# A two-block transformer kernel on one core: the front's first steps in another order

## The reference

```python
c_act = jax.nn.silu(c)
mod = c_act @ w_ada + b_ada                                # w_ada: 2048 x 6144
shift, scale, gate = jnp.split(mod, 3, axis=-1)
h = rms_norm(x, g) * (1.0 + scale[:, None]) + shift[:, None]
proj = jnp.einsum('bsd,df->bsf', h, w_in)                  # w_in: 2048 wide, chunks 0 to 9 of 512 columns in the front
```

## Time and profile before

| | |
|---|---|
| median of 3 runs | 1444.6 us (1443.38 to 1445.47) |
| the profiled execution's own time | 1443.75 us |
| its span | 1441.6 us |
| PE busy | 98% of the span |
| DVE busy | 83% |
| ACT busy | 49% |
| granted TensorE clock, mean | 0.996 |
| DMA over the span | 450.97 MB, mean 313 GB/s |

### The profile page before, as it was taken

The page is one execution under the profiler, slowest core; times in us unless marked ns, Lnnn a source line. Parts: engine busy times, 40 slices in busy tenths (PEclk is TensorE's granted clock), DMA queues, the critical chain, the costliest instruction groups (busy, mean ns, idle before and its releaser), DMA issues.

```text
span 1441.6 us, 19793 instructions
## 1 busy us (share of the span) xinstructions
PE 1406.3 (98%) x6934; PEld 1175.4 (82%) x6934; DVE 1191.0 (83%) x1533; ACT 708.5 (49%) x1039; POOL 139.9 (10%) x233
## 2 busy tenths in 40 slices
PE   6999999999999999999999999999999999999996
PEld 4778888878887788888888888878888888888885
DVE  6899899887999889898878789888887877677566
ACT  5564434754444644444455553464345545465440
POOL 1111011002100001110011101010010002110000
PEclk9999999999999999999999999999999999999999
DMA  9999999878997899999977799689789688775762
GB/s 355 411 412 416 411 404 385 311 284 280 403 415 259 288 347 379 406 377 359 347 237 255 239 343 406 195 279 360 262 338 345 209 311 270 231 252 173 266 194 97
DMA packets 101625, 450.97 MB, mean 313 GB/s; under 512 B 11730, under 2 KB 16162, under 8 KB 77858
## 3 DMA queue, kind: packets, MB, share of 16 engines
q1 hardware_dynamic: 68690, 247.63, 48.0%
q0 software_dynamic: 25584, 185.63, 33.4%
q10 hardware_dynamic: 7264, 16.55, 3.5%
HBM read 447.62 MB, written 2.15 MB: 312 GB/s over the span
## 4 chain that ended last, share of the span: by engine, by line
PE 84%; DVE 7%; DMA 4%; issue 3%; ACT 2%; POOL 0%; DVEq 0%; SPq 0%; ACTq 0%
PE bank L862 15%; PE bank L879 15%; PE bank L881 15%; PE bank L880 14%; PE bank L860 8%; DVE gw L1660 3%; PE bank L814 3%; PE bank L816 3%; PE bank L815 3%; DMA raw<-in_t_steps 3%; PE bank L1109 2%; PE bank L1067 2%; DVE w_lo L1652 2%; PE bank L858 1%; PE bank L827 1%
## 5 line engine op out<-in xcount | busy, mean ns | idle before, releaser
L1190 ACT CAST w_hi<-raw 128x1024 fp32r<-128x1024 f32 x436 | 457.4, 1051 | 610.0 <-PE bank L881 282.7
L1635 DVE TENSOR_TENSOR w_lo<-raw,w_hi 128x1024 fp32r<-128x1024 f32 x360 | 438.7, 1226 | 179.1 <-ACT w_hi L1190 177.7
L1660 DVE CUSTOM_DVE_ANT_0 gw<-gw,c_act 128x2048 f32<-128x2048 f32 x176 | 402.4, 2287 | 0.0
L880 PE MATMUL bank<-w_lo,act_parts 128*128 128x512 f32 x1024 | 398.9, 390 | 0.0
L879 PE MATMUL bank<-w_hi,act_parts 128*128 128x512 f32 x960 | 386.4, 403 | 0.5 <-issue 0.5
L881 PE MATMUL bank<-w_hi,act_parts 128*128 128x512 f32 x960 | 374.9, 391 | 0.0
L862 PE MATMUL bank<-act_parts,w_hi 128*128 128x512 f32 x960 | 338.3, 395 | 0.0
L860 PE MATMUL bank<-act_parts,w_lo 128*128 128x256 f32 x1024 | 276.9, 281 | 0.0
L880 PEld LDWEIGHTS bank<-w_lo,act_parts 128*128 128x128 f32 x1024 | 192.6, 188 | 38.2
L862 PEld LDWEIGHTS bank<-act_parts,w_hi 128*128 128x128 f32 x960 | 180.1, 188 | 39.1
L881 PEld LDWEIGHTS bank<-w_hi,act_parts 128*128 128x128 f32 x960 | 180.2, 188 | 38.8
(11 more groups left out here) (197 smaller groups left out, 1060.2 us busy)
## 6 DMA issues: line engine op xcount, KB each, us to landing
raw<-in_t_steps SPq DMA_DIRECT2D x464, 512.0 KB, 6.3
gw<-in_t_mod POOLq DMA_DIRECT2D x96, 1024.0 KB, 8.2
gw<-in_t_ada POOLq DMA_DIRECT2D x48, 1024.0 KB, 8.3
gw<-in_t_kv_mod POOLq DMA_DIRECT2D x32, 1024.0 KB, 8.0
area<-gate_rows ACTq DMA_DIRECT2D x3, 1024.0 KB, 13.3
bias<-forget_sums ACTq DMA_DIRECT2D x16, 192.0 KB, 5.7
area<-in_ln_g ACTq DMA_DIRECT2D x2, 1024.0 KB, 9.2
area<-in_ln_b ACTq DMA_DIRECT2D x2, 1024.0 KB, 13.0
```

The costliest lines, as they stand in the source:

```text
L880: nc.tensor.matmul(dst, hi, w_lo[:, j % SLOTS, k], start=False, stop=False)
L1190: nc.scalar.copy(w_hi[:, b], raw[:, j % SLOTS]).then_inc(hi_ready, 1)
L1635: nc.vector.tensor_tensor(w_lo[:, j % SLOTS], raw[:, j % SLOTS], w_hi[:, j % LEAD].bitcast(F32), ALU.subtract).then_inc(lo_ready, 1)
L1660: nc.vector.tensor_tensor_reduce(out=w, in0=w, in1=c_act[:].rearrange("p (t n) -> p t n", t=TT), scale=1.0, scalar=0.0, op0=ALU.mult, op1= ...
```

## The change

The tables of the front and a few places in the opening are written anew. The first step is now (2, 0), (4, 0), the second (0, 0), (1, 0), the third (3, 0), (5, 0): three steps of k-tile 0. Chunks 2 and 4 are parted after one k-tile in place of two, so their banks are closed with step 0. Then steps take two chunks of one k-tile in many places where they took one chunk of two k-tiles. The row blocks, low parts and shifts have other places; the first two row blocks wait for the spread of c in place of the first part of x; raw loads 0 to 3 wait for row block 0, and the fifth for block 2; block 2 is issued when block 1 has landed.

```diff
-PARTED = {0: 8, 1: 8, 2: 2, 4: 2, 3: 2, 5: 2, 8: 4, 6: 8, 9: 6, 7: 8}
-PART_BANKS = ({0: 0, 1: 1, 2: 2, 4: 3, 3: 2, 5: 3, 8: 2, 6: 3, 9: 2, 7: 2},
-              {2: 0, 4: 1, 3: 3, 5: 2, 0: 0, 1: 1, 8: 0, 9: 1, 6: 0, 7: 1})
-FRONT = [((0, 0), (1, 0)), ((2, 0), (4, 0)), ((2, 1), (4, 1)), ((0, 1), (1, 1))]
...
+PARTED = {0: 8, 1: 8, 2: 1, 4: 1, 3: 2, 5: 2, 8: 4, 6: 8, 9: 6, 7: 8}
+PART_BANKS = ({2: 0, 4: 1, 0: 2, 1: 3, 3: 0, 5: 1, 8: 0, 6: 1, 9: 0, 7: 0},
+              {2: 2, 4: 3, 3: 1, 5: 0, 0: 0, 1: 1, 8: 0, 9: 1, 6: 0, 7: 1})
+FRONT = [((2, 0), (4, 0)), ((0, 0), (1, 0)), ((3, 0), (5, 0)), ((3, 1), (5, 1)), ((0, 1), (1, 1)), ((8, 0), (8, 1)),
+         ((6, 0), (6, 1))]
+FRONT += [((p, kt), (q, kt)) for kt in (2, 3) for p, q in ((8, 6), (0, 1))]
...
+FRONT += [((2, 1), (4, 1))] + [((q, kt), (q, kt + 1)) for q in (2, 4, 3, 5) for kt in (2, 4, 6)]
+FRONT += [((p, kt), (q, kt)) for kt in range(8, KT) for p, q in ((2, 4), (3, 5))]
...
-ROW_AT = {4: 4, 5: 5, 6: 6, 7: 7, 8: 9, 9: 10, 10: 12, 11: 13, 12: 15, 13: 16, 14: 18, 15: 20}
-ROW_AT.update({g: 22 + int((g - 16) * 1.65) for g in range(16, HEAD_TILES)})
-LOW_AT = {1: 2, 2: 6, 3: 8, 4: 12, 5: 14, 6: 18, 7: 21}
+ROW_AT = {3: 2, 4: 4, 5: 5, 6: 6, 7: 8, 8: 10, 9: 11, 10: 13, 11: 14, 12: 16, 13: 18, 14: 20, 15: 21}
+ROW_AT.update({g: 23 + int((g - 16) * 1.65) for g in range(16, HEAD_TILES)})
+LOW_AT = {1: 3, 2: 6, 3: 9, 4: 12, 5: 15, 6: 19, 7: 22}
...
-SHIFT_AT = {1: 3}
-SHIFT_AT.update({kt: ROW_AT[2 * kt + 1] + (3 if kt < 8 else 2) for kt in range(2, KT)})
+SHIFT_AT = {1: 3, 2: 6, 3: 10, 4: 13, 5: 17, 6: 21, 7: 24}
+SHIFT_AT.update({kt: ROW_AT[2 * kt + 1] + 2 for kt in range(8, KT)})
...
             for k in range(FRONT_STEPS):
-                if k == 2:
+                if k == 0:
+
+                    sp.wait_ge(gw_landed[0], 16)
+                if k == LEAD:
 
                     sp.wait_ge(gw_landed[2], 16)
...
-            pool.wait_ge(x_begun, 16)
+            pool.wait_ge(c_spread, 2)
             load(0)
             load(1)
             inverse_root(("x",))
 
-            pool.wait_ge(raw_landed[0], 16)
+            pool.wait_ge(gw_landed[1], 16)
...
-                if n < 2:
-                    pe.wait_ge(head_kept, 4 * (n + 1))
...
+                    if n < 2:
+
+                        pe.wait_ge(head_kept, 2 * (bank_of(q, 0) + 1))
...
             head_step(0)
-            for r in range(6):
+            for r in range(2):
                 head_keep(r)
             head_kt(0)
-            for r in range(6, TURNS):
+            head_step(1)
+            for r in range(2, TURNS):
                 head_keep(r)
-            head_step(1)
...
+                gemv_step(0)
                 dve.wait_ge(root_ready, 1)
                 nc.vector.tensor_scalar(area[:, Q, 1], resid[:, 1], rstd[:, 1:2], None, ALU.mult
                                         ).then_inc(xhat_ready, 1)
+                gemv_step(1)
                 dve.wait_ge(vecs_landed, 16)
-                gemv_step(0)
-                gemv_step(1)
                 head_finish(0)
                 split_low(0)
                 head_low(0)
                 split_low(1)
                 gemv_step(2)
-                gemv_step(3)
-                head_finish(1)
```

More of the change, by code:

```diff
@@ new lines @@
+PART_BANKS = ({2: 0, 4: 1, 0: 2, 1: 3, 3: 0, 5: 1, 8: 0, 6: 1, 9: 0, 7: 0},
[3 more added lines that the diff above has]
+FRONT += [((p, kt), (q, kt)) for kt in (2, 3) for p, q in ((8, 6), (0, 1))]
+FRONT += [((9, kt), (9, kt + 1)) for kt in (0, 2)]
+FRONT += [((p, kt), (q, kt)) for kt in (4, 5) for p, q in ((9, 6), (0, 1))]
@@ L122 @@
+FRONT += [((7, kt), (7, kt + 1)) for kt in (0, 2, 4)]
+FRONT += [((p, kt), (q, kt)) for kt in (6, 7) for p, q in ((0, 1), (6, 7))]
+FRONT += [((2, 1), (4, 1))] + [((q, kt), (q, kt + 1)) for q in (2, 4, 3, 5) for kt in (2, 4, 6)]
+FRONT += [((p, kt), (q, kt)) for kt in range(8, KT) for p, q in ((2, 4), (3, 5))]
+FRONT += [((q, kt), (q, kt + 1)) for q in (0, 1, 8, 9, 6, 7) for kt in range(PARTED[q], KT, 2)]
 FRONT_STEPS = len(FRONT)
 HEAD_LEAD, LEAD_STEPS = 6, 24
-ROW_AT = {4: 4, 5: 5, 6: 6, 7: 7, 8: 9, 9: 10, 10: 12, 11: 13, 12: 15, 13: 16, 14: 18, 15: 20}
@@ L626, in _ @@
             sp.dma_start(vecs[:], a["t_vecs"]).then_inc(vecs_landed, 16)
-            sp.wait_ge(x_landed[1], 32)
             def decay_load(n):
@@ L1503, in head_x @@
                 spread_silu(1)
+                spread_silu(2)
                 act.wait_ge(x_begun, 16)
@@ L1507, in head_x @@
                                      accum_out=square_sums[:, 0:1]).then_inc(x_squared, 1)
-                spread_silu(2)
                 spread_silu(3).then_inc(silu_ready, 1)
@@ L1730, in front @@
                             head_low(kt)
-                    for g in range(4, HEAD_TILES):
+                    for g in range(3, HEAD_TILES):
                         if ROW_AT[g] == m:
```

## The result

| | before | after |
|---|---|---|
| median | 1444.6 us (9 runs, 1443.12 to 1448.76) | 1452.14 us (9 runs, 1450.23 to 1456.49) |
| the profiled execution | 1443.75 us, span 1441.6 | 1452.83 us, span 1451.0 |

After stands to before as 1.0051, with a 95% interval of 1.004 to 1.0062: the change costs 7.5 us. The forecast was 1442.2 with a range of 1439.6 to 1445.2, most likely no difference that can be told, and slower only with 0.06. It was wrong, on the side that I held least likely, and my slower rival is not what happened.

What follows compares the result with a forecast made beforehand. PE, busy 1406.3 of 1441.6 us, could win only idle or low-clock time, with full DMA engines bounding the front; the front's lead, cut to 2.4 us, took 1443.75 to 1441.3, median 1442.2, range 1439.6 to 1445.2.

Steps and rivals of the forecast that it cites:

- my slower rival: Opening: raw loads beside blocks 2 and 3 delay block 3's landing and so step 2; 1446.5 us at 31 us; chance 0.08.
- the rest: Other banks for the parts, PE's waits on kept copies, SP's removed wait on x: claimed to cost nothing.
- what is kept of it: Steps 52 to 61: bytes limit the lead, the hole gives 2.1 us; step 61 starts 2.0 to 3.0 earlier, 2.4 taken.
- The opening: Start of the front: x lands 0.8 us earlier, and step 0 starts at 21.0, 0.9 us earlier.
- The third step: Step 2, k-tile 0 again: waits for `parted` behind k-tile 1's scaling, starts at 31.5 against 32.05, pays 1.6 us low clock.
- the late variant: Opening: step 0's raw load late, delaying all by a microsecond; step 2 starts at 32.6, lead at step 8 is 1.6 us.
- K-tile 2: Steps 2 to 7: low part at 40.9 against 45.16, DVE wins about 4 us; steps end at 50.0, 2.7 us ahead.
- my own signs of being wrong: Step 2 right behind step 1, no longer wait near step 61, block 3 landing after 29, step 8's lead under 1 us.
- One k-tile a step: Middle of the front: only small stalls at steps 15 and 22; PE 3 to 4 us ahead at step 50.
- the cap by bytes: At step 52 bytes, not PE, bind: its load can land earlier only by the hole's 2.1 us, less a short dip.
- the first: Rival on the front's end: all of the 3 to 4 us stays, plus 0.7 at step 61; 1440.3 us; chance 0.27.
- The third: Rival on the opening: block 3 lands after some 29 us, each further microsecond delays step 2; 1446.5 us; chance 0.08.

Runs made afterwards that it cites:

- experiment 5: Changed kernel, but ACT copies the banks of chunks 2 and 4 before k-tile 1's pair: 1452.26 us, ratio 1.0051 to the kernel before.
- experiment 6: experiment 2 with the edit of experiment 5 (bank copies of chunks 2 and 4 ahead of k-tile 1's scaling): 1442.44 us, ratio 0.998.
- experiment 8: experiment 2 with the opening's transfers in the old order, row blocks and raw loads waiting as before: 1445.22 us, ratio 1.0004.
- experiment 9: experiment 2 with only SP's waits, which hold the raw loads, put back as before: 1445.1 us, ratio 1.0002.
- experiment 2: Changed kernel with the old bank table and k-tiles 8 to 15 again two at a time through one chunk: 1441.76 us, ratio 0.9981.
- experiment 1: Changed kernel with only the old table of banks put back: 1448.79 us, ratio 1.0025 to the kernel before.
- experiment 7: experiment 2 with the row blocks of steps 48 to 63 begun four steps later: 1443.25 us, ratio 0.9979.
- experiment 11: experiment 2 with the edits of experiment 5 and experiment 7 together: 1442.98 us, ratio 0.9986.

## Why the prediction was wrong

Point by point, by its own steps.

*The step that failed* is the one called **the rest**: "other banks for the parts [...] costs nothing: each is met when its neighbour is". I had asked for the waits on kept copies at the beginning of the front, where I looked at `parted` with care and found that step 2 stands behind k-tile 1's pair, and did not ask the same of `evacuated` at its end. The other half of the same mistake stands under **what is kept of it**: "adds now come in two steps of four in place of four of two, the same sum". The sum was right, 4.8 us for these four chunks' adds in both (a fifth chunk's two adds, at 197.70 in before, fall into the stretch too). But PE waits for one add in the list and not for the sum, and that one moved from the first place (177.4) to the last (185.7). No rival had it either. Measured, the two together are 10.4 us (1452.14 against 1441.76; 10.0 if each is taken against before's median in its own group), 3.4 for the banks and 7.0 for the order, taken away one after the other. The new banks with the old order were not run.

*The opening*: forecast 0.9 us earlier for step 0, measured later. It starts at 22.30 against 21.92. x did not land earlier by the row blocks' later start (DVE's square of its half is at 9.63 us in both), so the 0.8 us that I had estimated for it has no support in these traces. PE's 32 transposes began at 16.26 and took 6.29 us where they took 5.10. Why they took longer is not shown; in experiment 5, whose lists are the same up to there, they took 5.56 us and step 0 started at 21.36.

*The third step*: right in its mechanism, `parted` behind k-tile 1, which held step 2 until 33.06 (forecast 31.5, and 32.6 in the late variant). Block 3 was in time: DVE's work on it began at 27.22, straight after a split. Block 2 came at 23.86, for which DVE waited 1.75 us; that held back the split of step 2 and block 3 behind it, and is the size of the 1.6 us by which step 2 missed its forecast. The low clock cost more than taken: all twelve matmuls of the step ran at the slow pace, 33.06 to 38.3, where before it ended within the step.

*K-tile 2*: low part at 42.34, where 40.9 to 42.3 was forecast: right in the late variant. But steps 2 to 7 did not end at 50.0 (51.1 in the late variant): step 8 starts at 52.14 against 52.72, **0.6 us ahead where I had 2.7**. Of the 2.1 us missing, 1.6 are the later start of step 2, and its longer low clock accounts for the rest. A lead under 1 us at step 8 was one of my own signs of being wrong, and it came.

*One k-tile a step*: DVE's list in the middle of the front held as walked; PE was 1.3 to 1.9 us ahead in steps 11 to 52 wherever a cast that waits for PE tells it in both, where I had 3 to 4. What k-tiles 2 to 7 gain by it was not measured apart. Its end, k-tiles 8 to 15, is where the loss arises: alone on the kernel before it costs 5.0 us.

*What is kept*: experiments 5, 6, 8 and 9 and the table bear out the cap by bytes, and with the bank wait taken away the sum came out at its size: 2.4 us forecast, 2.5 measured (0.9981). That the size fits so well is in part luck, since its terms do not. The hole at 16 to 19 us was filled, but 0.2 MB or so of it only moved, to 14 to 16 us (338 GB/s where before had 393) and 8 to 10. The load of step 52 was cast at 167.35 in place of 168.34, 1.0 us earlier where I had 2.1 and more, in the profiled execution. Nor did the surplus go where I had it go: PE's waits between steps 53 and 61 in experiment 2 are 0.63 and 0.65 us, not 1.5 to 2.

*The rivals*: the first (the gain survives to the end) found no support: more lead than the bytes give never came out in a median. The third, block 3 landing late, did not occur. As for the rule of the Trainium skill ("DMA: Bandwidth & Descriptors", Queues, rings and completion order) that each engine takes turns between its queues: the trace of after agrees. Block 2, now with raw loads beside it, took 8.5 us from issue to landing where it took 5.2 before; that is the slower rival in a milder form, 1.75 us of DVE's time and no more. As for the low clock: experiment 5 keeps the granted clock at 1.00 in 28 to 40 us, where after has 0.72, but the wait and the low clock then fall on step 5, and the time stays the same.

## What to carry to other kernels

When a change moves where accumulators close, go through each opening of a new part and ask which closed one its banks come from, at which place in the adding engine's list that one is read, and when that place is reached in the trace of before: here the answer, adds that end at 186.6 us against a start at 177.8, was in rows of a trace already at hand. Equal sums of work on an engine say nothing about the one item in its queue that another engine waits for. And where the transfers look like the bound of a stretch, as here, it was the edits that start transfers earlier that paid, and a PE that waited less was no gain by itself.

## What the runs showed of the hardware

The slow pace behind a wait of PE does not last in proportion to the wait. The clock of 1.2 GHz (matmuls of 0.63 us in place of 0.39) held for about 5.3 us behind 5.04 us idle in after, for 3.3 us behind 5.06 us in experiment 2, for 3.7 us behind 7.63 us in experiment 8, for 2.9 us behind 9.31 us at step 53, and for 5.7 us behind 3.93 us in experiment 5 and 4.28 us in experiment 1. In the forecast I took 1.6 us for it whatever the wait; with a matmul every 0.43 us in place of 0.23 these stretches cost 1.4 to 2.7 us.

The same code of the opening moved between 18.47 and 19.23 MB by 50 us in the profiled executions that have it, 1.8 us of traffic at 414 GB/s apart. A single trace could not have ranked experiments 2, 6, 7 and 11, and neither can their medians.
